# A shared expert's down products, cut into units of 256 columns inside the loop over expert passes

## The reference

```
def body(acc, blk):                      # per expert, on the tokens that chose it
    hb = jax.nn.silu(xb @ w_gate[eb]) * (xb @ w_up[eb])
    yb = hb @ w_down[eb]
    return acc.at[tok_b].add((yb * gate_b[:, None]).astype(acc.dtype)), None
shared = (jax.nn.silu(x2 @ w_sh_gate) * (x2 @ w_sh_up)) @ w_sh_down
return acc[:T] + shared                  # ffn
x = layer_norm(DEEPNORM_ALPHA * x + ffn, ln2_g[i], ln2_b[i])
```

## Time and profile before

| what | value |
|---|---|
| median of three runs | 1965.85 us |
| the profiled execution | 1966.91 us |
| its span, first to last instruction | 1965.2 us |
| mean granted TensorE clock | 0.977 of full speed |
| TensorE busy | 1791.4 us (91%) |
| VectorE, ScalarE, GpSimd busy | 753.3, 379.9, 354.6 us |
| read from memory over the span | 521.58 MB |

### The profile page before, as it was taken

One profiled execution on the slowest core, in us unless ns is written; L12 is line 12 of the kernel. 1 busy time (PEld: TensorE's weight loads), 2 busy tenths in 40 slices (PEclk: granted clock), 3 DMA queues, 4 the chain that ended last, 5 costly groups with the idle time before them and its releaser, 6 DMA issues. The chain is left out here.

```text
span 1965.2 us, 36205 instructions
## 1 busy us (share of the span) xinstructions
PE 1791.4 (91%) x12636; PEld 1111.3 (57%) x12637; DVE 753.3 (38%) x2180; ACT 379.9 (19%) x870; POOL 354.6 (18%) x450
## 2 busy tenths in 40 slices
PE   9999999889999989879999979999879999997877
PEld 7888445456666555543344458754446666664442
DVE  4222754633333223225255653416523333332225
ACT  2111651011111111102365143201001111110001
POOL 8442000011111111110022722100111111111110
PEclk9999999999999999999999979899999999999999
DMA  6220225599999999998123220207898999999997
GB/s 228 79 80 23 97 97 210 223 412 420 422 420 422 421 421 421 421 420 329 57 62 78 63 42 3 87 1 295 327 407 368 421 421 421 420 421 422 422 415 309
DMA packets 144184, 541.80 MB, mean 276 GB/s; under 512 B 31030, under 2 KB 68498, under 8 KB 94302
## 3 DMA queue, kind: packets, MB, share of 16 engines
q1 hardware_dynamic: 122782, 490.20, 62.4%
q0 software_dynamic: 21312, 50.37, 6.6%
HBM read 521.58 MB, written 46.14 MB: 289 GB/s over the span
## 5 line engine op out<-in xcount | busy, mean ns | idle before, releaser
L718 PE MATMUL bank<-W,XT 128*64 128x256 f32 x2880 | 327.0, 383 | 37.8 <-DMA W<-in_w_exp_up_dram 17.5
L718 PEld LDWEIGHTS bank<-W,XT 128*64 128x64 f32 x2880 | 234.2, 138 | 140.7 <-DMA W<-in_w_exp_gate_dram 26.2
L755 PE MATMUL bank<-W,ht 128*64 128x512 f32 x720 | 167.5, 607 | 14.0 <-DMA W<-in_w_exp_down_dram 8.6
L2260 PE MATMUL bank<-XT,room 128*128 128x512 f32 x352 | 158.7, 605 | 0.0
L729 DVE TENSOR_TENSOR sig<-sig,bank 128x256 f32<-128x256 f32 x72 | 30.4, 422 | 270.6 <-ACT sig L725 270.5
L718 PE MATMUL bank<-room,XT 128*64 128x256 f32 x864 | 103.2, 392 | 18.0 <-issue 9.7
L731 DVE TENSOR_TENSOR h<-sig,bank 128x256 f32<-128x256 f32 x72 | 30.4, 422 | 217.4 <-PE bank L718 217.4
L2260 PEld LDWEIGHTS bank<-XT,room 128*128 128x128 f32 x352 | 66.3, 193 | 82.2 <-issue 81.9
L784 POOL DMA_INDIRECT y_rows<-y,row x36 | 36.8, 1021 | 419.9 <-DVE y L777 419.9
L784 POOL DMA_INDIRECT y_rows<-XT,row x36 | 36.4, 1012 | 420.2 <-DVE XT L777 420.2
L704 ACT ACTIVATE XT<-bank 128x512 f32<-128x512 f32 x74 | 44.2, 597 | 334.8 <-PE bank L696 334.8
(11 more groups left out here) (491 smaller groups left out, 2781.3 us busy)
## 6 DMA issues: line engine op xcount, KB each, us to landing
W<-in_w_exp_gate_dram SPq DMA_DIRECT2D x88, 1024.0 KB, 25.2
W<-in_w_exp_up_dram SPq DMA_DIRECT2D x88, 1024.0 KB, 27.3
W<-in_w_exp_down_dram SPq DMA_DIRECT2D x88, 1024.0 KB, 26.8
room<-in_w_exp_gate_dram SPq DMA_DIRECT2D x40, 1024.0 KB, 22.8
third_high<-in_w_exp_down_dram SPq DMA_DIRECT2D x40, 1024.0 KB, 24.7
W<-y_rows SPq DMA_DIRECT2D x24, 1024.0 KB, 13.2
third_up<-in_w_exp_up_dram SPq DMA_DIRECT2D x20, 1024.0 KB, 25.9
w_shg<-in_w_exp_up_dram SPq DMA_DIRECT2D x20, 1024.0 KB, 22.9
```

Source lines behind the costliest of these rows:

```text
L718: last = pe.matmul((gate, up)[m][64 * a:64 * a + 64, :], xt[s][:, k, 64 * a:64 * a + 64], weights(w, a, m)[:, k * FE:(k + 1) * FE], start= ...
L755: last = pe.matmul(B[5 + half][64 * a:64 * a + 64, :], ht[:, j, 64 * a:64 * a + 64], weights(w, a, 2)[:, at:at + 512], start=(j == 0), sto ...
L2260: last = pe.matmul(main(i)[:], wc[i % WBUFS][:, kb, :], K.XT[:, kb, :], start=(kb == 0), stop=(kb == KD - 1))
```

## The change

The shared down product is taken out of `Combination` and cut into 16 units: one tile of 128 tokens by 256 columns each. At the head of each of the turns 1 to 17, before TensorE reads the slot, `shared_product` does two matmuls of 256 columns (one for each half of the contraction) into the bank of the up product. VectorE adds the result to X times a factor (`add_shared`). ScalarE prepares each unit at the end of the pass with `u` = 1 (`stage_hidden`): it reads from the table `due` whether a unit falls to the coming turn (a turn that has none gets a factor of 1 and hidden activations times zero), computes the factor (1 or ALPHA), and copies the 128 x 256 hidden activations of the unit. In this run turns 3 to 17 carry 15 units; the last one is done at the start of `Combination` (`shared_rest`).

The shared down weights (1 MiB) are loaded at the head of SyncE's loop into their own buffer instead of near its end. For room in on-chip memory, the routed results keep one buffer instead of two (`keep_y` of pass n waits for the scatter of pass n - 1), `sig` and `h` are one buffer, and constants that serve only to make other constants move into memory that is used later for something else (the mask `masks4` becomes `masks3`, `head_cols` holds two columns of `heads`). In `Combination` the multiplication of X by ALPHA goes, and the first row product of a tile starts the bank.

```diff
+UNITS = 16
+UNIT = NT * D // UNITS
...
+    K.due = sb("due", [P, MAX_PASSES - UNITS], BF16)
...
-    K.plan_turns = sb("plan_turns", [1, 1], I32)
+    K.plan_turns = sb("plan_turns", [1, 2], I32)
...
-                step.inc(dve.tensor_copy(K.plan_turns[:], gsum[0:1, 0, :]))
+                step.inc(dve.tensor_copy(K.plan_turns[:, 0:1], gsum[0:1, 0, :]))
+                step.inc(dve.tensor_scalar(K.plan_turns[:, 1:2], gsum[0:1, 0, :], -1.0, float(MAX_PASSES // 2), ALU.mult, ALU.add))
...
-        y = [xt_room[:, 0:D], sb("y1", [P, D])[:]]
+        y = xt_room[:, 0:D]
...
-        sig, h = sb("sig", [P, FE]), sb("h", [P, FE])
+        h = sb("h", [P, FE])
...
+        sh_down = sb("w_sh_down_kept", [P, 2 * D])
+        staged_hidden = sb("staged_hidden", [P, 2, P])
+        due, factor = sb("due_now", [P, 1]), sb("factor_now", [P, 1])
...
+            before = eng.value_load(K.plan_turns[0:1, 1:2], min_val=0, max_val=MAX_PASSES // 2 - UNITS)
             for u in range(2):
-                body(u, u)
+                body(u, u, 0, before)
             turns = eng.value_load(K.plan_turns[0:1, 0:1], min_val=PAIRS // 2, max_val=MAX_PASSES // 2)
             with eng.Fori(1, turns) as turn:
                 for u in range(2):
-                    body(turn * 2 + u, u)
+                    body(turn * 2 + u, u, turn, before)
+
+        FIRST_DUE = UNITS - (MAX_PASSES // 2 - UNITS + 1) % UNITS
+
+        def unit_bits(turn, before, bits):
+            return (before + (turn + FIRST_DUE)) & bits
+
+        def stage_hidden(act, turn, before):
+            wait_from(act, shared_added, turn)
+            act.activation(due[:], K.due[:, bass.ds((before + (turn + 1)) & 63, 1)], ACT.Copy).then_inc(due_kept, 1)
+            act.wait_ge(due_kept, turn + 1)
+            act.activation(factor[:], due[:], ACT.Copy, bias=1.0, scale=ALPHA - 1.0)
+            at = unit_bits(turn + 1, before, UNITS - D // UNIT) * (P * UNIT // D)
+            act.activation(staged_hidden[:], shared.hidden[:, :, bass.ds(at, P)], ACT.Copy, scale=due[:, 0:1]).then_inc(hidden_staged, 1)
+
+        def shared_product(pe, n, turn, before):
+            pe.wait_ge(shared.loaded, 16)
+            pe.wait_ge(hidden_staged, turn)
+            pe.wait_ge(hidden_done, n)
+            at = unit_bits(turn, before, D // UNIT - 1) * UNIT
+            for j in range(2):
+                last = pe.matmul(up, staged_hidden[:, j, :], shared.w[:, j, bass.ds(at, UNIT)], start=(j == 0), stop=(j == 1))
+            last.then_inc(shared_made, 1)
+
+        def add_shared(dve, turn, before):
+            dve.wait_ge(shared_made, turn)
+            x = X_flat[:, bass.ds(unit_bits(turn, before, UNITS - 1) * UNIT, UNIT)]
+            dve.scalar_tensor_tensor(x, x, factor[:], up, ALU.mult, ALU.add).then_inc(shared_added, 1)
...
+                if m == 1 and s == 0 and not isinstance(n, int):
+                    pe.wait_ge(shared_added, shared_turn)
...
-            wait_from(act, hidden_done, n)
+            wait_from(act, h_turned, n)
             act.wait_ge(gate_done, n + 1)
-            act.activation(sig[:], gate, ACT.Sigmoid).then_inc(sigmoid_done, 1)
+            act.activation(h[:], gate, ACT.Sigmoid).then_inc(sigmoid_done, 1)
 
         def hidden(dve, n, step):
             dve.wait_ge(sigmoid_done, n + 1)
-            step(dve.tensor_tensor(sig[:], sig[:], gate, ALU.mult))
+            step(dve.tensor_tensor(h[:], h[:], gate, ALU.mult))
             dve.wait_ge(gate_up_done, n + 1)
-            dve.tensor_tensor(h[:], sig[:], up, ALU.mult).then_inc(hidden_done, 1)
+            dve.tensor_tensor(h[:], h[:], up, ALU.mult).then_inc(hidden_done, 1)
...
-            wait_from(eng, stored[s], through(n - 2, s))
+            wait_from(eng, stored[1 - s], through(n - 1, 1 - s))
             eng.wait_ge(down_done, 2 * n + 1 + half)
-            dst = y[s][:, half * 512:half * 512 + 512]
+            dst = y[:, half * 512:half * 512 + 512]
...
+                shared.load_down(sp, sh_down[:])
...
+                    if u == 0 and not early:
+                        shared_product(pe, n, shared_turn, before)
...
+                    if u == 1:
+                        stage_hidden(act, turn, before)
...
+                    if u == 0 and not isinstance(n, int):
+                        add_shared(dve, turn, before)
...
-        self.shared.load_down(sp, self.down_room)
...
-    def shared_product(self, pe, t):
-        B, shared = self.K.banks, self.shared
-        for half in range(2):
-            for j in range(2):
-                pe.matmul(B[2 * t + half][:], shared.hidden[:, j, t * P:(t + 1) * P], shared.w[:, j, half * 512:(half + 1) * 512],
-                          start=(j == 0), stop=False)
...
-                                 start=False, stop=(q == ROW_PAIRS - 1))
+                                 start=(q == 0), stop=(q == ROW_PAIRS - 1))
...
-    def products(self, pe):
+    def shared_rest(self, pe):
         pe.wait_ge(self.shared.loaded, 16)
+        for j in range(2):
+            last = pe.matmul(self.K.banks[7][:, 0:UNIT], self.shared.hidden[:, j, T - P:T], self.shared.w[:, j, D - UNIT:D],
+                             start=(j == 0), stop=(j == 1))
+        last.then_inc(self.rest_made, 1)
+
+    def products(self, pe, y_a, y_d, passes):
+        self.shared_rest(pe)
         for t in range(2):
-            self.shared_product(pe, t)
             self.row_product(pe, t, 0)
             self.row_product(pe, t, 1)
-        pe.wait_ge(self.scaled, 1)
         self.row_product(pe, 0, 2)
         self.row_product(pe, 1, 2)
-        self.shared_product(pe, 2)
-        self.row_product(pe, 2, 0)
-        self.row_product(pe, 2, 1)
-        self.row_product(pe, 2, 2)
-        self.shared_product(pe, 3)
+        for y_kept in (y_a, y_d):
+            pe.wait_ge(y_kept, 1)
+            pe.wait_ge(y_kept, passes)
+        pe.wait_ge(self.rest_added, 1)
+        for q in range(ROW_PAIRS):
+            self.row_product(pe, 2, q)
...
+        dve.wait_ge(self.rest_made, 1)
+        x = X[:, NT - 1, D - UNIT:D]
+        dve.scalar_tensor_tensor(x, x, ALPHA, B[7][:, 0:UNIT], ALU.mult, ALU.add).then_inc(self.rest_added, 1)
+        dve.wait_ge(self.rest_added, 1)
         for t in range(NT):
-            dve.tensor_scalar_mul(X[:, t, :], X[:, t, :], ALPHA).then_inc(self.scaled, 1)
-        for t in range(NT):
-            dve.wait_ge(self.scaled, t + 1)
```

More of the change, by code:

```diff
@@ L108, in constants, with carve @@
     K.causal = sb("causal", [P, P], BF16)
-    K.upto = sb("upto_f32", [P, P])
-    K.ones = sb("ones_f32", [P, P])
-    K.heads = sb("heads", [P, P])
-    K.masks4 = sb("masks4", [P, 4 * P], BF16)
-    K.level = sb("level", [P, 7, P], BF16)
+    made_in = K.arena[:, 4 * TOKW // P * T:4 * TOKW // P * T + NMH // 2 * T]
+    at = [0]
+    def carve(n, dt):
+        size = n * mybir.dt.size(dt) // mybir.dt.size(F32)
+        at[0] += size
+        return made_in[:, at[0] - size:at[0]].bitcast(dt)
+    K.upto = carve(P, F32)
+    K.heads = sb("heads", [P, P], BF16)
+    K.head_cols = sb("head_cols", [P, 2])
+    K.masks3 = sb("masks3", [P, 3 * P], BF16)
+    K.level = carve(7 * P, BF16).rearrange("p (l t) -> p l t", l=7)
+    K.due = sb("due", [P, MAX_PASSES - UNITS], BF16)
     K.blocks = sb("blocks", [P, P // BW, BW], BF16)
@@ L210, in make @@
             step(pool.tensor_tensor(K.level[:, lv, :], K.level[:, lv, :], K.upto[:], ALU.mult))
-        for q in range(4):
-            step(pool.tensor_copy(K.masks4[:, q * P:(q + 1) * P], (K.upto if q % 2 else K.before)[:]))
+        for q in range(3):
+            step(pool.tensor_copy(K.masks3[:, q * P:(q + 1) * P], (K.before if q % 2 else K.upto)[:]))
         for t in range(NT):
@@ L623, in expert_loop @@
         gates_turned = sem("gates_turned")
+        due_kept, hidden_staged, shared_made, shared_added = (
+            sem(n) for n in ("due_kept", "hidden_staged", "shared_made", "shared_added"))
         steps = sem("steps")
@@ L706, in keep_xt, with gate_up @@
                 eng.tensor_copy(dst, B[1][:]).then_inc(xt_d, 1)
-        def gate_up(pe, s, n, turn, w):
+        def gate_up(pe, s, n, turn, w, shared_turn):
             pe.wait_ge(xt_a, n + 1)
@@ L837, in _, with one_pass @@
                 gather(pool, 1, 1)
-                def one_pass(n, u):
+                def one_pass(n, u, turn, before):
                     read = held(pool, 2 * (n + 1))
@@ L857, in _, with one_pass @@
                 slot_rows(pe, 1, 1)
-                def one_pass(n, u):
+                def one_pass(n, u, shared_turn, before):
                     early = isinstance(n, int)
+                    if u == 0 and not early:
+                        shared_product(pe, n, shared_turn, before)
                     slot = None if early and n == 0 else entry(pe, K.plan_slot, n, WSLOTS - 1)
@@ L864, in from_slot @@
                     def from_slot(w):
-                        gate_up(pe, u, n, turn, w)
```

(4 more changed lines are left out.)

17 lines of the change are left out of this document (9 added, 8 removed).

## The result

The changed kernel takes 1995.96 us (median of 4 runs, 1994.0 to 1999.82) against 1966.8 us (1964.68 to 1968.91) for the kernel before: a ratio of 1.0155, 95% interval 1.0134 to 1.0177. It is slower by 29 us; forecast were 19.

A forecast was written before the change was run, and what follows sets the result against it. TensorE and weight transfers were both taken as nearly full: transfers set the loop ends, TensorE the middle. 17.0 + 9 - 2.7 - 4.2 = +19 us gave 1985 us on the median, 1.0% slower, range 1968 to 2003 us.

The forecast's parts named there:

- The first rival: TensorE's sequencer is not held by the staging wait, so a turn costs only 0.9 us: 1963 us, chance 0.08.
- x: Time TensorE loses per turn at the gate products, from the staging wait and the sequencer work behind it: 2.8 us.
- Layer 1: 17.0 forecast: Layer 1's expert loop: the weight queue restarts 17.0 us late, and transfers set the end behind that as before.
- 10x - 11.0: Layer 1's queue restart: ten turns' delay before the refill at 1696.4, less 11.0 us of transfers ahead of it: 17.0 us.
- Layer 0: 9 forecast: Layer 0's expert loop ends 9 us later, as queue restart and TensorE's pace are both near limits.
- the larger of the two limits: In layer 0 each pass pays the later of queue restart, 6.9 us late, and TensorE's pace, 8.1 us late.
- the slack of 39.5 us: Layer 0's loop end at 892.4 against 852.9 for 34 passes of 12.82 us from pass 2, TensorE alone.
- The ends: -4.2 and -2.7 forecast: Combination after each expert loop gets shorter without the shared matmuls: 4.2 us in layer 0, 2.7 us in layer 1.
- The rival by which the ends win all of TensorE's share: Combination bound by TensorE throughout saves 21.8 us over both layers; with 0.9 us per turn, 1948 us; chance 0.04.
- Nothing for the one buffer: Single result buffer costs nothing: scatters land by 1575.9 at the latest, before the copy, with 1.5 us to spare.
- Nothing for the early 1 MiB: Loading shared down weights at the queue's head, 2.6 us of transfer, costs nothing since the queue later stands still longer.
- The clock rival: Granted clock falls at each turn's matmul gaps, time above 2004 us; chance 0.07 together with the one-buffer rival.

The follow-up runs named there:

- early staging: Changed kernel with ScalarE's staging of the next unit moved ahead of its copy of the down product in odd passes: 1975.37 us, ratio 1.0052.
- shifting the old kernel: Kernel before with 30 long-satisfied semaphore waits on TensorE ahead of the first pass of each layer, loop unchanged: 1962.57 us, ratio 1.0002.
- slot 2 first: Staging moved ahead of ScalarE's down-product copy in the changed kernel, plus the even pass's three copies in order 2, 1, 0: 1973.79 us, ratio 1.0038.
- reads first: Changed kernel with the two table reads (slot and turn) ahead of the shared product, staging still late: 1979.65 us, ratio 1.0079.
- both: Changed kernel with staging ahead of the down-product copy and the table reads ahead of the shared product: 1978.05 us, ratio 1.0065.
- the four with the product behind the hidden tile: Changed kernel, staging earlier, shared product after turning the hidden tile: 1964.33 us; copies ordered 2, 1, 0: 1962.48; 0, 1, 2: 1964.15; that plus never-entered code: 1965.88.
- Without the shared work: Changed kernel without staging, product and addition per turn; one run, only layer 0 read: loop 505.2 us, end 46.5 us.

## Why the prediction was right, and where its terms were off

**Direction and cause: right.** The wait for the staged tile holds the sequencer, and what stands behind it lies bare. The first rival, the sequencer not held, is out: the register operation behind the wait comes at 1572.3, after the staging's end at 1572.20, and with the staging early x falls to 1.2 us. The prediction set this against what the Trainium skill, "Perfetto Trace Analysis", Tensor Engine Instruction, says of a matmul with a wait: it is pushed into a wait queue, and the sequencer is ready for the next instruction. That rule does not bear on this wait, which stands on an instruction of the sequencer's own ahead of the matmuls (L690), and the trace does not speak against it: with early staging the sequencer reads `plan_slot` at 1563.7, while the product's matmuls, issued before the read, start at 1565.96.

**x: 2.8 forecast, 3.05 measured.** From the start of the down products: end of staging 3.54 us (forecast 3.7; the two small copies take 0.2 us each, not 0.26), from there to the reads 0.7 (forecast 0.35: a semaphore instruction, five register operations and the two matmuls take twice what I gave them), reads to gate products 2.2 (2.05), start 0.07 (0.1). Less 3.46. The step that was mis-sized is the issue of the product. "Of which only 0.9 us are work" is wrong: the sum has no such term, and cutting the work to 0.60 us of matmuls left the start of the gate products where it was. The first rival's 0.9, the product alone, is 1.2 with early staging.

**Layer 1: 17.0 forecast, 20.0 measured.** The queue went as forecast: its restart came at 1735.1 instead of 1696.4 + 11.0, 27.7 us later, of which 8.1 are the later start of the layer; 19.6 are left, and 10x - 11.0 with x = 3.05 is 19.5. What failed is "behind that the transfers set the end as before": from 1495 us to the end of the loop TensorE waits for no transfer. I had worked out TensorE's slack for layer 0 only. In layer 1 the passes 27 to 35 of before stand 33.4 us above 12.81 each, and 17x - 33.4 = 18.5 us. Passes 0 and 1 add 1.8 us (13.00 and 16.00 against 12.70 and 14.54) and the turn with the lower clock 1.8; passes 2 to 5, which stall in both kernels, take 1.4 less than their two turns would add, and the other turns, a little under 3.05 us each, 0.6 less: 20.0. That the queue's 19.6 is so near is chance; TensorE's limit with x = 2.8 would have been 14.2.

**Layer 0: 9 forecast, 20.2 measured.** TensorE sets it, as the larger of the two limits said, but the slack of 39.5 us was too large: it took pass 2 of before at full pace, where the gate products ran at a lower clock (0.71 from 417.03 to 426.50) and lost 3.0 us. The passes 18 to 35 of before stand 36.5 us above 12.81 each; 17x - 36.5 with the measured x is 15.4. The stall at pass 4 adds 20.80 - 12.81 - 3.0 = 5.0 us, a term that the prediction did not have at all. Pass 0 is 1.5 us longer (13.75 against 12.21). Pass 2, stalled in both, is only 0.9 us longer, 2.1 less than a turn, and 0.4 us are spread over the rest. The stall does not belong to the change's idea: shifting the old kernel makes the same one.

**The ends: -4.2 and -2.7 forecast, -8.6 and -1.0 measured.** Where the transfers still set the end of layer 0's loop (early staging, also with slot 2 first, reads first, both, and the four with the product behind the hidden tile) its end is 4.3 to 5.2 us shorter: about the forecast. Without the shared work it is 3.3. In the changed kernel the loop ends with no transfer of weights left, so that the rows of the first two tiles were there, and 32 matmuls on them ran in one go (beside the earlier trace rows; TensorE, layer 0):

```profile
912.23 1.13 PE L1067 MATMUL bank<-w_sh_down_kept,sh_h 128*128 128x256 f32 x4
913.34 7.09 PE L1058 MATMUL bank<-W,w_shg 128*64 128x512 f32 x32
922.68 1.94 PE L1058 MATMUL bank<-W,w_shg 128*64 128x512 f32 x8 [2.25 <-DMA W<-y_rows]
```

In layer 1 the rows come later than in the earlier trace rows, and nearly every row product waits for its own; the last:

```profile
L1029 SPq DMA_DIRECT2D W<-y_rows x12: 359/469/2271, 1942.8 to 1960.5; - x12
...
DMA to landing us min/median/max: 4.8/12.5/20.8
```

```profile
1981.47 1.94 PE L1058 MATMUL bank<-W,w_shg 128*64 128x512 f32 x8 [1.74 <-DMA W<-y_rows]
```

The last pair lands at 1981.3, 34.9 us behind the last down product; before it was 1951.9, 33.5 us behind. The late loads eat 1.4 of the 2.7 us. The rival by which the ends win all of TensorE's share, 21.8 us, is out: they won 9.6.

**Between the loops,** -3.3 us: nothing of the change runs there. The window 1200 to 1280 has a mean granted clock of 0.89 before and 0.96 after; in eleven of the twelve other kernels this part takes 464.5 to 466.3 us, in one 461.7, also with a clock of 0.96. It varies without the edit, and with the clock; why is open.

**Nothing for the one buffer: right,** shown by the kernel before with one buffer. Scatters land after 8.2 us, at most 9.7 (8.1 and 9.6). **Nothing for the early 1 MiB** holds for the loop that the transfers set. But pass 0 of layer 0 is 1.5 us longer in the changed kernel and also without the shared work, and not with one buffer alone; where TensorE sets the end, as in the changed kernel, that counts. Whether it is the early load or another of the small edits is not shown.

**The clock rival** came about in one of the 30 steady turns (0.55, 1.8 us); in the others the clock behind the gap was 1.00. One column instead of 256 brought it on in most: the margin was thin.

With the measured terms the sum is 20.2 - 8.6 - 3.3 + 20.0 - 1.0 - 0.2 (start) = +27.1. That this misses the forecast of +19 by no more than 8 us is in part luck: the loops came out 14.2 us above their forecasts, and 4.4 us of layer 0's end and the 3.3 us between the loops took back more than half of that.

## What to carry to other kernels

A wait that holds a sequencer costs what stands behind it: the reads, addresses and branches that used to run under the engine's work. Before adding work at the head of a loop, make its condition true early, or put it behind the reads and where the engine already waits; here that took the price of a turn from 3.05 to 0.53 us. And compare the first passes on their own, down to the sequencer's branches: here code that did not touch the loop moved a stall of 7 to 8 us from one layer to the other.

## What was not expected of the hardware

- 30 instructions ahead of a loop, each a wait long satisfied, moved a stall of about 7 to 8 us (4.8 to 5.2 us idle, the rest slower matmuls behind it) from layer 1 to layer 0. The stall is one branch of TensorE's sequencer that takes 5.7 to 6.1 us and 0.29 us where there is none.
- With 0.60 us of matmuls between gaps of 0.5 and 1.8 us the granted clock behind them was 0.58, and a turn took 1.6 us longer than with 1.13 us between gaps of 0.5 and 1.3 us, where it was 1.00 in 29 of 30 steady turns. In the one left, with the same gaps, it was 0.55.
